# Attention steps placed between projections, output products and merge products, on one core

## The reference, cut to what matters

```python
# second mixer (layer 1 of the first block): 16 heads of 64
q, k, v = split(xn @ w_in)                       # three times 1024 columns
sc = q . k over an 8 x 16 grid neighbourhood + rpb bias
h = h + (softmax(sc) @ v) @ w_out

# second block: three mixers of the same hn, merged by gates
gates = sigmoid(p_gate)                          # (.., 3, 1024)
merged = gates[0] * (y_a @ w_branch_rwkv) + gates[1] * (y_b @ w_branch_pool) + gates[2] * (y_c @ w_branch_attn)
x = x + merged @ w_out                           # y_c: attention of 8 heads over all 512 tokens, 2 key heads
x = x + expert_choice_ffn(rms_norm(x))           # 16 experts
```

## Time and profile before

| what | value |
|---|---|
| three runs | 3315.34, 3319.7, 3321.82 us, median 3319.7 |
| profiled execution | span 3318.4 us from first to last instruction; what lies around it is not recorded, and the median of the runs is 1.3 us above the span |
| PE, PE weight loads, DVE, ACT, POOL busy | 97%, 74%, 46%, 32%, 9% |
| granted PE clock | 0.994 in the mean |
| DMA | 448.77 MB, mean 135 GB/s, 425 GB/s in the experts |

### The profile page before, as it was taken

One profiled execution on the slowest core, in us unless ns is written; L12 is line 12 of the kernel. 1 busy time (PEld: TensorE's weight loads), 2 busy tenths in 40 slices (PEclk: granted clock), 3 DMA queues, 4 the chain that ended last, 5 costly groups with the idle time before them and its releaser, 6 DMA issues. The chain is left out here.

```text
span 3318.4 us, 46903 instructions
## 1 busy us (share of the span) xinstructions
PE 3219.3 (97%) x20286; PEld 2468.8 (74%) x20286; DVE 1527.3 (46%) x2217; ACT 1068.0 (32%) x1596; POOL 308.7 (9%) x365
## 2 busy tenths in 40 slices
PE   9999999999999999999999999979999999989988
PEld 7888887888888888889788888758877888434332
DVE  5443556644435544332754434685567544201112
ACT  4222226432224322222732223553344323200001
POOL 1000131200001000000300001211111301100000
PEclk9999999999999999999999999989999999999999
DMA  4222441122233222332222222301010323899998
GB/s 144 102 90 90 145 143 40 39 102 89 90 96 113 102 89 90 96 107 108 84 97 94 98 88 98 106 20 49 3 65 20 105 99 124 345 427 425 425 427 336
DMA packets 62799, 448.77 MB, mean 135 GB/s; under 512 B 8705, under 2 KB 10369, under 8 KB 32641
## 3 DMA queue, kind: packets, MB, share of 16 engines
q1 hardware_dynamic: 62592, 445.76, 35.9%
HBM read 438.39 MB, written 2.10 MB: 133 GB/s over the span
## 5 line engine op out<-in xcount | busy, mean ns | idle before, releaser
L569 DVE TENSOR_TENSOR w_lo<-slot,w_hi 128x2048 fp32r<-128x2048 f32 (+4 forms) x243 | 487.1, 2005 | 331.6 <-ACT w_hi L560 329.3
L167 PE MATMUL bank<-xa,w_hi 128*128 128x512 f32 x1368 | 535.9, 392 | 1.2 <-DVE w_lo L3170 1.1
L168 PE MATMUL bank<-xa,w_hi 128*128 128x512 f32 x1368 | 532.4, 389 | 0.0
L169 PE MATMUL bank<-xa,w_lo 128*128 128x512 f32 x1368 | 532.3, 389 | 0.0
L560 ACT ACTIVATE w_hi<-slot 128x2048 fp32r<-128x2048 f32 (+4 forms) x243 | 406.1, 1671 | 335.5 <-PE bank L169 326.3
L167 PE MATMUL bank<-xb,w_hi 128*128 128x512 f32 x832 | 324.7, 390 | 0.7 <-DVE w_lo L569 0.6
L168 PE MATMUL bank<-xb,w_hi 128*128 128x512 f32 x832 | 323.7, 389 | 0.0
L169 PE MATMUL bank<-xb,w_lo 128*128 128x512 f32 x832 | 323.7, 389 | 0.0
L167 PEld LDWEIGHTS bank<-xa,w_hi 128*128 128x128 f32 x1368 | 256.8, 188 | 63.1 <-issue 5.4
L169 PEld LDWEIGHTS bank<-xa,w_lo 128*128 128x128 f32 x1368 | 256.8, 188 | 53.8
L168 PEld LDWEIGHTS bank<-xa,w_hi 128*128 128x128 f32 x1368 | 256.8, 188 | 53.4 <-issue 1.2
(11 more groups left out here) (511 smaller groups left out, 4872.4 us busy)
## 6 DMA issues: line engine op xcount, KB each, us to landing
slot<-in_w_gu SPq DMA_DIRECT2D x87, 1024.0 KB, 4.7
slot<-in_exp_gate SPq DMA_DIRECT2D x25, 2048.0 KB, 15.2
slot<-in_exp_up SPq DMA_DIRECT2D x24, 2048.0 KB, 15.0
slot<-in_exp_down SPq DMA_DIRECT2D x24, 2048.0 KB, 15.8
slot<-in_w_dn SPq DMA_DIRECT2D x64, 704.0 KB, 4.0
slot<-in_w_gate SPq DMA_DIRECT2D x24, 768.0 KB, 4.3
xe<-in_exp_up SPq DMA_DIRECT2D x8, 2048.0 KB, 13.4
xe<-in_exp_down SPq DMA_DIRECT2D x8, 2048.0 KB, 15.2
```

The source lines that it names most:

```text
L167: e.matmul(out, w[0], x[0], start=(j == 0), stop=False)
L168: e.matmul(out, w[0], x[1], start=False, stop=False)
L169: return e.matmul(out, w[1], x[0], start=False, stop=(j == n - 1))
L569: dve.e.tensor_tensor(lo, slot(k, b), hi.bitcast(F32), ALU.subtract).then_inc(L.up("w_lo", b))
```

## The change

In the second mixer only the first two head pairs are projected ahead of the attention. The other 12 projections and all 16 value products become pieces, one behind the scores of each PE step 0 to 27. Blocks are reordered (pair, pair, values, four times). Steps 28 to 36 hold parts of the first three output products, on three banks kept back; part (n, lo, hi) takes operands lo to hi-1. The attention writes to tiles of its own (`m.out`), no longer over the mixer's input.

In the third part the attention moves into the merge: pieces 0 to 15 are gate and branch products of branch 0 for the 8 column tiles in turn, then gate (0, 1), the pool products, branch (0, 1), gate (0, 2). `yr` is made ahead of the attention. The rest of the merge follows in the old way. Weight slots 2 and 3 no longer serve the merge.

```diff
+def c_block(k, t):
+    return k.first["c"] + 3 * (t // 2) + t % 2
+def c_ahead(k, t):
+    return k.first["c"] + 3 * (t // 8) + {0: 3, 4: 4, 6: 5}[t % 8] if t % 8 in (0, 4, 6) and t <= 28 else None
+def c_piece(t):
+    if not 0 <= t < 28:
+        return None
+    g, p = (t + 4) // 8, (t + 4) % 8
+    return ("v", t // 8, t % 8) if t % 8 < 4 else ("qk", 2 * g + p // 2, p % 2)
+C_OUT_PARTS = {28: ((0, 0, 4),), 29: ((1, 0, 4),), 30: ((2, 0, 4),), 31: ((0, 4, 5), (1, 4, 5)), 32: ((2, 4, 5),),
+               33: ((0, 5, 6), (1, 5, 6), (2, 5, 6)), 35: ((0, 6, 7), (1, 6, 7)), 36: ((2, 6, 7),)}
...
 def pe_c(k, nm, nx):
-    pe_heads(k, "c", nm, k.xa, [(b["c_qk"] + j, 2) for j in range(8)], None, lambda: pe_norm(k, nm))
+    def between(t):
+        piece = c_piece(t)
+        if piece and piece[0] == "v":
+            g, i = piece[1:]
+            pe_value(k, "c", g, i, k.first["c"] + 3 * g + 2, 256, k.xa, key_tile, ("edge_hi", "edge_lo"), m.xe)
+        elif piece:
+            project(*piece[1:])
+        for n, lo, hi in C_OUT_PARTS.get(t, ()):
+            out_part(n, lo, hi)
+    for t in range(2):
+        for z in range(2):
+            project(t, z)
+            if t == z == 0:
+                pe_norm(k, nm)
     pe_rstd_turn(k, "c", nm)
-    for g in range(4):
-        pe_values(k, "c", g, b["c_v"] + g, 256, k.xa, key_tile, ("edge_hi", "edge_lo"), k.c.xe)
-    pe_attention(k, "c", m.att, c_units(k))
-    pe_out(k, "c", nx, b["c_out"], k.xa, lambda i: ("att_out", "c", 4 * i + 3))
+    pe_attention(k, "c", m.att, c_units(k), between)
+    for n in range(3):
+        out_part(n, 7, KT)
+    for n in range(3, KT):
+        out_part(n, 0, KT)
...
+AX_PIECES = [(kind, i, 0) for i in range(KT) for kind in ("gate", "branch")] + [("gate", 0, 1), ("mix", 0, 1), ("branch", 0, 1), ("gate", 0, 2)]
+AX_REST = [("branch", 0, 2)] + [(kind, i, z) for i in range(1, KT) for z in (1, 2) for kind in ("gate", "branch")]
...
 def act_merge(k, nx):
+    def between(t):
+        if 0 < t <= len(AX_PIECES):
+            kind, i, z = AX_PIECES[t - 1]
+            if kind == "gate":
+                sigmoid(i, z)
+            if kind == "mix":
+                act_pool_mix(k)
+        if t < 18 and t % 2 == 0:
+            act_weight(k, k.first["w2_gate"] + t // 2 + 1)
+        if t == 19:
+            act_weight(k, gate_block(k, 1, 1))
...
 def dve_merge(k, nx):
+    def between(t):
+        if t == 0:
+            for j in range(4):
+                dve.wait_ge(*L.at("yr_hi", j))
+                y = col(k.y_rwkv, j)
+                e.tensor_tensor(m.yr[j][1], y, m.yr[j][0].bitcast(F32), ALU.subtract).then_inc(L.up("yr_lo", j))
+        if 0 < t <= len(AX_PIECES):
+            kind, i, z = AX_PIECES[t - 1]
+            if kind == "mix":
+                dve_pool_mix(k)
+            else:
+                (scaled if kind == "gate" else gated)(i, z)
+        if t < 18 and t % 2 == 0:
+            dve_weight(k, k.first["w2_gate"] + t // 2 + 1)
...
-    sp_weights(k, f["c_v"])
+    sp_weights(k, f["c"] + 2)
     for h in range(4):
         sp_c_bias(k, h)
-    sp_weights(k, f["c_out"] + 2)
-    for h in range(4, 16):
-        sp_c_bias(k, h)
+    for t, upto in enumerate((6, 8, 9, 11, 12, 14)):
+        sp_weights(k, f["c"] + upto)
+        for h in (2 * t + 4, 2 * t + 5):
+            sp_c_bias(k, h)
...
+        if b == k.first["w2_gate"]:
+            slots.remove(3)
+        if b == k.first["exp"]:
+            slots = [2, 3] + sorted(slots)
+            held[2] = held[3] = ("mg_lo", 7)
```

More of the change, by code:

```diff
@@ L1259, in act_c @@
+def act_c(k, nm, nx, gain):
+    m, b = k.c, k.first["c"]
+    def between(t):
+        piece = c_piece(t - 1)
+        if piece and piece[0] == "v":
+            g, i = piece[1:]
+            act_value(k, "c", g, i, 256, lambda i: m.v[:, i, g * 256:(g + 1) * 256], lambda i: m.rT[:, i:i + 1], 0)
+        if c_ahead(k, t) is not None:
+            act_weight(k, c_ahead(k, t))
+    act_weight(k, b + 1)
     act_root(k, nm, k.rstd_last, True)
[L1260 to L1263, removed]
+    act_weight(k, b + 2)
+    act_edges(k, nm)
@@ L1264, in act_c @@
     k.rstd_last = ("rstd_turned", "c", 0)
[L1265 to L1271, removed]
-def dve_c(k, nm, nx, gain):
[L1275 to L1282, removed]
-        dve.wait_ge(*L.at("rstd", nm))
-        e.scalar_tensor_tensor(out=dst[i], in0=k.banks.of("proj", "c", i)[:, :], scalar=0.125 if i < 8 else 1.0, in1=k.rstd,
-                               op0=ALU.mult, op1=ALU.mult).then_inc(L.up("proj_out", "c", i))
+    act_table(k, "exp_c", ACT.Exp)
@@ L1286, in dve_c @@
     dve_rstd_turn(k, "c", m.rT)
[L1287 to L1290, removed]
+    dve_attention(k, "c", m.att, c_units(k), between)
+    dve_out(k, "c", nx, k.first["c_out"], gain, k.xb, {1: 2, 4: 3, 6: 4})
 def sp_ple(k, layer):
@@ L2550, in pe_merge, with piece @@
     ys = [(m.yr, lambda j: ("yr_lo", j)), (k.y_pool, lambda j: ("ypool_lo", j)), (k.y_att, lambda j: ("att_out", "ax", 4 * j + 3))]
[L2551 to L2554, removed]
+    def piece(kind, i, z):
+        if kind == "mix":
+            pe_pool_mix(k)
+            return
+        b = gate_block(k, i, z)
+        w = views(part(k, b), "p (k c) -> p k c", k=12)
+        if kind == "gate":
             pe.wait_ge(*L.at("w_lo", b))
@@ L2617, in dve_merge @@
+    dve_attention(k, "ax", k.ax.att, ax_units(k), between)
+    gated(0, 2)
+    for i in range(1, KT):
+        for z in (1, 2):
+            dve_weight(k, gate_block(k, i, z) + 1)
+            scaled(i, z)
+            if (i, z) == (7, 2):
                 for j in (1, 2, 3):
                     split(j)
-            dve.wait_ge(*L.at("gate2_sigmoid", i, z))
-            dve.wait_ge(*L.at("branch", i, z))
-            e.tensor_tensor(sg if z else m.mg[i], sg, k.banks.of("branch", i, z)[:, :], ALU.mult).then_inc(L.up("branch_gated", i, z))
@@ L2622, in dve_merge @@
[L2622 to L2627 removed]
+            gated(i, z)
         if i == 4:
```

212 lines of the change are left out of this document (139 added, 73 removed).

## The result

The kernel after takes 3335.1 us (median of four runs, 3333.6 to 3339.9) against 3318.7 us of the kernel before beside it (3315.3 to 3321.8): 1.0056 times as long, 95% interval 1.0044 to 1.0068, which is 15 to 23 us. The profiled execution took 3334.6 us, with a span of 3333.3.

What follows compares the result with a forecast made beforehand. TensorE was taken to be bound by product-form changes rather than waits in its attention steps. +6 us (second mixer) and +9 (third part) on a span of 3318.4 give 3333.4, median 1.3 above: 3334.7 us, range 3317 to 3346.

Steps and rivals of the forecast that it cites:

- Three changes a step ... 0.2 each: Attention steps on TensorE: three product-form changes a step cost some 0.55 us, 0.2 each, not idle time work can fill.
- Gained: the ramp: Second mixer's attention: 1.7 us of its 65.8 is waiting, which the pieces would fill, -1.7 us.
- The end of the mixer: Second mixer: steps 35 and 36 add 0.7 us; output parts waiting for unit 31, with little cover, add 1.3 us.
- I take zero, up to 1 us late: After the second mixer's attention: conversion of output weights (block 2) behind three outputs costs nothing, at most 1 us.
- C: Stretch from the second mixer's first product to the next feed-forward's first product; forecast +6 us, bounds +3 to +8.
- even step "no wait", odd step 1.3: Third part's attention: gate pieces (even) wait for nothing; branch pieces (odd) wait 1.3 us for an Exp behind a table load.
- 0.85 waited in step 2: Third part's attention, step 2: TensorE waits 0.85 us for yr, a sigmoid, a table load and the Exp.
- I take +9: Third part's attention: 64.6 against 54.3 us, +10, taken as +9 since first weights partly overlap the wait; bounds +1, +14.
- Passes whole: After the merge: experts are bound by their start, so the loss passes on whole to the end.
- 1 (gaps are hidden): Both attentions: TensorE's gaps are issue and waiting that queued pieces hide; -17 and about +5, 3308 us; chance 0.13.
- 2 (half price): Both attentions: form changes cost half and ScalarE keeps up; +3 and +2, 3325 us, no difference; chance 0.14.
- 3 (each load or block costs 1.4 us more): Third part: TensorE waits 1.4 us longer for the bank in six odd steps and step 2; 3344 us; chance 0.15.

Runs made afterwards that it cites:

- the alternating order: Kernel after with pieces moved between transposes and scores; then every odd step of the second mixer's first 28 reversed, its tail re-ordered: 3326.1 us, ratio 1.0023 to the kernel before.

## Why the prediction was right

The verdict and both mechanisms hold, and the size is near: +15 forecast, 16.5 between the medians, 15 to 23 by the interval, 18.6 in the two changed stretches. That the profiled execution came out at 3334.6 against 3334.7, and the median at 3335.1, is luck in part: each part was sized about 2 us too low, and in the profile the stretch between gained 3.5.

- **"Three changes a step ... 0.2 each", not idle time.** Right. The extra changes cost 0.20 us a step in the second mixer (steps 5 to 27, +4.6 us), 0.19 came back when they were taken away, and 0.15 was lost when they were added elsewhere. I had taken 0.17, "a little under the 0.2": 0.7 us too little over these steps, 0.2 more over steps 28 to 31. The Trainium skill, TensorEngine Tiling (Array Packing), Tiling Modes, says that a changed mode drains the engine. The runs agree, in that a change costs 0.15 to 0.20 us with the next product queued.
- **"Gained: the ramp", -1.7.** Missed by 0.6 us net. Steps 0 to 4 took 5.02 us beside their pieces, 5.16 before; I had -1.7 and +1.0 for their new changes. So there was next to nothing to gain in the ramp; how much of its 5.16 us was waiting the runs don't tell.
- **The end of the mixer.** 0.7 for steps 35 and 36 and 1.3 for the split were forecast, and about 1.4 came for both. The output weights, "I take zero, up to 1 us late", were 0.9 late (1.1 by the starts of the products), but not the block that the argument was about: the third was in time, the fourth was not. This is the clearest mis-sized term. The runs with another split order didn't cure it: the third block a tile earlier made the fourth 3.8 us late, the fourth a tile earlier left PE waiting for the third. So C +8.05 against +6.
- **Third part, even step "no wait", odd step 1.3.** Right: 3.54 and 4.90 us beside the piece, forecast 3.5 and 4.8, and six waits of 1.28. The cause is shown from both sides, by taking away the loads and by taking another bank.
- **"0.85 waited in step 2".** No such wait is in the list: steps 0 to 4 took 8.2 us beside their pieces, 8.6 forecast. Steps 5 to 15 took 47.1 against 46.3, and step 17, with the pool products, 2.7 against 2.26.
- **"I take +9", from +10.** This is the term of the third part that missed. The steps' own sum, 64.6 against 54.3, was near (65.4 measured, of which 0.6 came back where before had lost it around the pool products, so +10.6); the allowance for first weights overlapping the wait had no row behind it.
- **Passes whole.** From the first output product of the merge to the end it is 549.8 us before and 549.0 after, so nothing of the loss was made up there: other runs, with the same products from there on, have 549.1 to 554.2.
- **Rivals.** 1 (gaps are hidden) and 2 (half price) fell by the runs with one change less and one more. 3 (each load or block costs 1.4 us more) fell: the load starts 0.02 us after the copy and the Exp 0.01 after the load. The drain, which the Trainium skill (ScalarE: Activation LUTs, What ACT_TABLE_LOAD costs) puts at 1380 ns, is not seen here; its 1283 ns for the load are, seventeen times.

What stays open: why a change costs 0.15 us in one place, 0.16 in a pair and 0.19 to 0.20 beside a piece, and where the alternating order's missing 0.17 comes from.

## What to carry to other kernels

Before work is put between the steps of a pipeline on TensorE, look at which gaps are waits and which are borders between product forms: here only the first kind could be filled, and each insertion should sit next to a product of its own form. A shared ring of banks is part of the order of work: ask which reader frees the bank that the inserted product will get, and what stands ahead of that reader. Cover is worth something only if it is spent, here on issuing two units at a time, which without the cover gave nothing.

## What the runs showed that I had not expected

The stretch between C and T, the same instructions in every kernel here, took from 823 to 828 us in the profiles (828 with the wait of 1.1 us at its start). Most of it can be seen in the granted clock. Windows of PE (us, busy, instructions, clock, DMA share, GB/s) at the end of a stretch of short products, of before and of after:

```profile
2419.00:2439.00 20.00, 17.29 (x333) 0.91 0.27 94
```

```profile
2428.00:2448.00 20.00, 17.29 (x279) 1.00 0.30 107
```

PE is equally busy in both (17.29 of 20 us), and before it the work is the same; yet in one execution the clock goes down to its lower level (0.50, so 1.2 in place of 2.4 GHz, in the 2 us from 2431) and in the other it stays up. That is, as an estimate, 0.09 x 20 = 1.8 us of the 3.5. The other half lies in the recurrent mixer: over 60 us from 2200 the clock is 0.83 in the mean in before, and 0.86 over the same work in after (from 2208.6), which by the same estimate is 1.8 us again. Over the whole stretch the mean granted clock is 0.986 in before's profile and in five more, which took 826.4 to 826.6 us, and 0.990 in after's and in two more, which took 823.1 to 824.3. So profiles, which are single executions, can differ by some 3 us for reasons that have nothing to do with a change. C and T agree far better where nothing was changed: C is 243.72 and 243.70 us in the two profiles with the old second mixer, T 253.73 or 253.74 in the five with the old third part.
